# Prompt attention: TensorE multiplies the values of the item two back before it turns the weights of the last item

## Chip, core and metric

The kernel runs on one core of one Trainium2 chip. The metric is the device time of one execution in microseconds (us), as the median of several executions. One execution was also recorded by the hardware profiler, and every row below comes from that one.

## What is computed

The program is one layer of a decoder: a projection, two attention branches, their merge, and a mixture of experts, for a prompt of 512 tokens and a sample group of 32 tokens. The change touches only the attention of the prompt. Cut to that:

```python
# branch a: 8 query heads, 2 key/value heads, the top keys of an index score are kept
logits = einsum('bqgrd,bqkgd->bqgrk', qg, k_sel) * HEAD_DIM ** -0.5
p = softmax(where(valid, logits, -inf));  o_a = einsum('bqgrk,bqkgd->bqgrd', p, v_sel)
# branch b: 8 query heads, 8 key/value heads, blocks of 256 keys, causal inside the own block
p = softmax(concatenate([s_sel, s_own]));  o_b = p_own @ v_own + p_sel @ v_sel
```

With 512 keys the kernel treats both as dense attention with an additive mask: the index scores (with the dropped keys lowered) for branch a, a causal triangle for branch b. HEAD_DIM is 64, and a tile of queries has 128 rows.

## The kernel before

The program is a sequence of stages, each a block of instruction streams for the five engines, and a stage starts when all engines have ended the one before. `prompt` is the attention of the prompt; `project` is ahead of it, and `sample`, `merge`, `project_out` and `experts` are behind it. No instruction of another stage runs on an engine while `prompt` runs.

`prompt` works through 32 items. An item is one pair of heads (j = 0 to 3) of one branch ("b" or "a") for one tile of 128 queries (t). Four items make a group, which shares one output bank and one normalisation. The groups are, in order, b3, a3, b2, a2, b1, a1, b0, a0: the tile t = 3 sees 512 keys, t = 2 sees 384, t = 1 sees 256 and t = 0 sees 128, so items get shorter. Group g holds the items 4g to 4g+3.

The steps of an item m, by short names that the rest of the document uses:

- S(m), TensorE, line 1042: the scores of both heads (`scores`), into one of two pairs of banks.
- D(m), VectorE, lines 1145 and 1148: adds the mask and takes the row maximum.
- E(m), ScalarE, line 1104: the exponentials of both heads, with their sums. D(m) releases it.
- T(m), TensorE, line 1055: turns the weights (`turn`), 2(t+1) transposes of 128x128 into banks 4 and 5. It needs E(m), and the banks empty again, that is K(m-1).
- K(m), ScalarE (line 1114 for a b item, 1116 for an a item) and for b items VectorE too (line 1167): copies the turned weights out of the banks to `probT`. It needs T(m).
- W(m), TensorE, line 1069: multiplies the values with the turned weights (`weigh`), 2(t+1) products into bank 6. It needs K(m); the first item of a group also needs N of the group before, which empties bank 6.

Per group g there are four more:

- I(g), VectorE, line 1152: the reciprocals of the sums.
- P(g), TensorE, line 1081: spreads the reciprocals over the rows of bank 7 by 8 products (`spread`).
- X(g), ScalarE, line 1122: copies them out.
- N(g), VectorE, line 1158: multiplies bank 6 by them and writes the output; it needs X(g) and the group's last W.

Each engine runs its stream in the order in which it is written, and semaphores order the engines among each other. ScalarE's order in turn m of the loop is E(m), K(m-1), and X(g) behind K(m-1) where m = 4g+5. VectorE's is D(m), the copy of K(m-1) for a b item, I(g) where m = 4g+4, N(g) where m = 4g+5. GpSimd issues loads for the next stage when certain exponentials have been made. TensorE's order is what the diff changes.

Of the kernel before, what the change touches and what calls it, by code (L numbers as in the profile page):

```python
# [176 lines left out]
def const(s, name, rows=P):  # L177
    a, n = AT[name]
    return s.consts[0:rows, a:a + n]


def build(nc, a, o):

    with ExitStack() as ctx:
# [18 lines left out]
        with ExitStack() as attn:  # L203
# [7 lines left out]
            with ExitStack() as samp:  # L211
# [10 lines left out]
                with ExitStack() as qkv:  # L222
                    def sq(name, shape, dt=F32):
                        return qkv.enter_context(nc.sbuf_tensor(name, shape, dt, side="right"))
                    s.qaT = sq("qaT", [P, PAIRS, SEQ])
                    s.qbT = sq("qbT", [P, PAIRS, SEQ])
                    s.kbT = sq("kbT", [P, PAIRS, SEQ])
                    s.vbP = sq("vbP", [P, TP, H, HD])
                    s.vaP = sq("vaP", [P, TP, 2, HD])
                    s.score = sq("score", [P, TP, SEQ])  # L230
                    with nc.cleanup_on_exit():
                        project(nc, s, a, o)

                    s.oaT = sa("oaT", [P, PAIRS, NTOK])
                    s.obT = sa("obT", [P, PAIRS, NTOK])
                    s.bw = sa("branch_w", [P, 2, 2, PAIRS, P])
                    s.ring = samp.enter_context(nc.sbuf_tensor("ring", [P, NR, SLOT_B * QW], F32))
                    with nc.cleanup_on_exit():  # L238
                        prompt(nc, s, a)
# [726 lines left out]
def prompt(nc, s, a):  # L966
# [4 lines left out]
    with ExitStack() as ctx:  # L971
# [19 lines left out]
        n = len(ITEMS)  # L991

        def width(t):
            return (t + 1) * P


        def by_scalar(m):
            return sum(1 if item[1] == "b" else 2 for item in ITEMS[:m])

        def by_vector(m):  # L1000
            return sum(item[1] == "b" for item in ITEMS[:m])

        @block.gpsimd
        def _(pool):
            link = Chain(pool, queries_laid)
            keys = a["cache_k_idx"][0].rearrange("g (p e) d -> (g p) (e d)", e=SLOT)
            for half in range(2):
                r = slice(half * HD, half * HD + HD)
                link(nc.gpsimd.tensor_copy(s.q_a[r, :, half * 16:half * 16 + 16].rearrange("p b (j q) -> p b j q", q=NQ),
                                           s.qaS[r, :, :].rearrange("p j (b q) -> p b j q", q=NQ)))  # L1010
                for j in range(PAIRS):
                    c = (2 * j + half) * NQ
                    link(nc.gpsimd.tensor_copy(s.q_b[r, :, j, c:c + NQ], s.qbS[r, j, :].rearrange("p (b q) -> p b q", q=NQ)))
                for odd in range(2):
                    dst = s.q_i[r, :, :].rearrange("p b (j a q) -> p a b j q", a=2, q=NQ)
                    src = s.qiS[odd * HD:(odd + 1) * HD, :, :].rearrange("p j (b q) -> p b j q", q=NQ)
                    link(nc.gpsimd.tensor_copy(dst[:, odd, :, :, :], src))

            for k in range(NIDX):
                for u in range(4):  # L1020
                    b, f = 4 * (k // 2) + u, k % 2
                    pool.wait_ge(exp_done, 2 * (4 * k + u + 1))
                    pool.indirect_dma_start(s.ring[:, k, u * SLOT * HD:(u + 1) * SLOT * HD], None, keys,
                                            bass.IndirectOffsetOnAxis(s.rows[:, 2 * b + f:2 * b + f + 1], 0))\
                        .then_inc(s.arrived[k], 16)
            for n in range(NR - NIDX):
                pool.wait_ge(exp_done, 2 * (4 * NIDX + 3 * n + 2))
                gather_unit(pool, s, a, n)

        @block.tensor  # L1030
        def _(pe):
            ident = const(s, "ident")

            def scores(m):
                _, kind, t, j = ITEMS[m]
                if m >= 2:
                    pe.wait_ge(exp_done, 2 * (m - 1))
                for half in range(2):
                    r = slice(half * HD, half * HD + HD)
                    qT = s.qaT if kind == "a" else s.qbT  # L1040
                    kT = s.kaT[r, 0:width(t)] if kind == "a" else s.kbT[r, j, 0:width(t)]
                    last = nc.tensor.matmul(bank[:, 2 * (m % 2) + half, 0:width(t)], qT[r, j, t * P:(t + 1) * P], kT,
                                            start=True, stop=True)
                last.then_inc(qk_done, 1)

            def turn(m):
                t = ITEMS[m][2]
                pe.wait_ge(exp_done, 2 * (m + 1))
                for half in range(2):
                    if m >= 1:  # L1050
                        pe.wait_ge(tr_kept, by_scalar(m))
                    if by_vector(m):
                        pe.wait_ge(tr_kept_v, by_vector(m))
                    for c in range(t + 1):
                        last = nc.tensor.transpose(bank[:, 4 + half, c * P:(c + 1) * P],  # L1055
                                                   prob[:, m % 3, half, c * P:(c + 1) * P], ident)
                last.then_inc(tr_done, 1)

            def weigh(m):
                g, kind, t, j = ITEMS[m]  # L1060
                pe.wait_ge(tr_kept, by_scalar(m + 1))
                if by_vector(m + 1):
                    pe.wait_ge(tr_kept_v, by_vector(m + 1))
                if j == 0 and g >= 1:
                    pe.wait_ge(out_kept, g)
                for c in range(t + 1):
                    for half in range(2):
                        v = s.vaP[:, c, half, :] if kind == "a" else s.vbP[:, c, 2 * j + half, :]
                        last = nc.tensor.matmul(bank[half * HD:half * HD + HD, 6, j * P:(j + 1) * P], v,
                                                probT[:, m % 2, half, c * P:(c + 1) * P],  # L1070
                                                start=(c == 0), stop=(c == t))
                last.then_inc(weighed, 1)

            def spread(g):

                pe.wait_ge(inv_ready, g + 1)
                if g >= 1:
                    pe.wait_ge(wide_kept, g)
                for j in range(PAIRS):
                    for half in range(2):  # L1080
                        last = nc.tensor.matmul(bank[half * HD:half * HD + HD, 7, j * P:(j + 1) * P],
                                                inv[:, g % 2, j, half:half + 1].to_broadcast([P, HD]), ident,
                                                start=True, stop=True)
                last.then_inc(wide_done, 1)

            for m in range(n + 2):
                if m < n:
                    scores(m)
                if 1 <= m < n + 1:
                    turn(m - 1)  # L1090
                if m >= 2:
                    if (m - 1) % PAIRS == 0:
                        spread((m - 1) // PAIRS - 1)
                    weigh(m - 2)

        @block.scalar
        def _(act):
            def exps(m):
                g, _, t, j = ITEMS[m]
                for half in range(2):  # L1100
                    act.wait_ge(top_done, m + 1)
                    if m >= 3:
                        act.wait_ge(tr_done, m - 2)
                    nc.scalar.activation(prob[:, m % 3, half, 0:width(t)], bank[:, 2 * (m % 2) + half, 0:width(t)],  # L1104
                                         ACT.Exp, bias=ntop[:, m % 4, half:half + 1],
                                         accum_out=sums[:, g % 2, j, half:half + 1]).then_inc(exp_done, 1)

            def keep_turned(m):
                _, kind, t, _ = ITEMS[m]
                act.wait_ge(tr_done, m + 1)  # L1110
                if m >= 2:
                    act.wait_ge(weighed, m - 1)
                if kind == "b":
                    nc.scalar.copy(probT[:, m % 2, 0, 0:width(t)], bank[:, 4, 0:width(t)]).then_inc(tr_kept, 1)
                else:
                    nc.scalar.copy(probT[:, m % 2, :, 0:width(t)], bank[:, 4:6, 0:width(t)]).then_inc(tr_kept, 2)
# [1536 lines left out]
```

## Time and profile before

| | |
|---|---|
| median of 3 executions | 1060.63 us (1059.89 to 1061.24) |
| the profiled execution: its time | 1053.66 us |
| the profiled execution: first to last instruction | 1051.9 us |
| `prompt`, first score product to last normalisation | 183.62 to 286.90 us |
| TensorE busy over the span | 907.5 us, 86% |

The profiled execution was 7 us shorter than the median of the others, so durations are taken from the profile and differences are applied to the median. The profile shows an engine's instructions in order of time with their durations, and, in brackets, how long the engine had been idle and which engine's instruction released it. A TensorE row that stands for several matmuls gives the time from the start of the first to the end of the last; the next burst can start some 0.1 us before that end, as they are pipelined. (TensorE makes an fp32 product in passes, so the trace has twice as many matmuls as the program in S, W and P.)

### The profile page before, as it was taken

How to read it: one execution, taken by the hardware profiler on the slowest of the kernel's cores; microseconds unless marked ns; L12 is line 12 of the kernel's file. 1: busy time of each engine (PE TensorE's matmuls, PEld its weight loads, DVE VectorE, ACT ScalarE, POOL GpSimd, SP SyncE). 2: the span in 40 equal slices, each digit the busy share in tenths (PEclk: the TensorE clock that was granted, in tenths of full speed). 3: DMA queues.
4: the chain of work that ended last, by engine and by line, in shares of the span. 5: the costliest groups of instructions: out<-in, count | busy, mean ns of one | idle time of the engine just before them, and what ended most of it. 6: DMA issues, size and time to landing. Idle time of an engine off the chain costs nothing. (4 is left out here: it accounts for less than half of the span.)

```text
span 1051.9 us, 14867 instructions
## 1 busy us (share of the span) xinstructions
PE 907.5 (86%) x5957; PEld 581.6 (55%) x5957; DVE 429.8 (41%) x906; ACT 303.1 (29%) x542; POOL 198.6 (19%) x214
## 2 busy tenths in 40 slices
PE   6999998878699999989979999999659999777750
PEld 4775886555566666534669999744533444322220
DVE  4728996656428595312035422111341111111106
ACT  5435332455536776621300000011201111100002
POOL 0333330321012334423510000000111111011010
PEclk9999999899989999999989999999759999999995
DMA  9220221223267997999956550195359999999946
GB/s 327 94 92 1 94 71 43 61 61 117 85 221 261 341 372 306 356 411 354 395 185 177 184 185 21 26 341 205 109 206 395 414 413 413 414 413 414 404 167 238
DMA packets 87844, 246.87 MB, mean 235 GB/s; under 512 B 13088, under 2 KB 40928, under 8 KB 75360
## 3 DMA queue, kind: packets, MB, share of 16 engines
q1 hardware_dynamic: 66448, 144.45, 37.0%
q0 software_dynamic: 20560, 99.24, 25.0%
q10 hardware_dynamic: 768, 2.23, 0.6%
q8 instruction: 48, 0.79, 0.3%
q14 instruction: 20, 0.16, 0.0%
HBM read 238.50 MB, written 15.77 MB: 242 GB/s over the span
## 5 line engine op out<-in xcount | busy, mean ns | idle before, releaser
L1337 PEld LDWEIGHTS bank<-consts,ring 128*128 128x128 f32 x704 | 78.1, 143 | 38.6 <-ACT kT_s L1580 36.3
L1580 ACT COPY kT_s<-bank 128x1024 f32<-128x1024 f32 (+1 forms) x90 | 85.5, 996 | 45.7 <-PE bank L1337 45.7
L2357 PE MATMUL bank<-early,obT 128*64 128x512 f32 x352 | 82.0, 614 | 14.6 <-DMA early<-in_w_e_up 13.3
L1337 PE MATMUL bank<-consts,ring 128*128 128x128 f32 x704 | 89.5, 281 | 2.4 <-PEq L238 1.9
L2565 DVE TENSOR_TENSOR uT<-uT,bank 128x256 f32<-128x256 f32 x16 | 6.7, 421 | 182.2 <-ACT uT L2414 182.2
L491 POOL TENSOR_TENSOR w_lo<-w_raw,w_hi 128x512 fp32r<-128x512 f32 x37 | 49.1, 1329 | 105.0 <-ACT w_hi L534 105.0
L878 PE MATMUL bank<-w_hi,hT_hi_p 128*128 128x512 f32 x160 | 65.4, 408 | 0.0
L2357 PEld LDWEIGHTS bank<-early,obT 128*64 128x64 f32 x352 | 27.7, 141 | 66.8 <-issue 53.3
L878 PE MATMUL bank<-w_lo,hT_hi_p 128*128 128x512 f32 x160 | 62.5, 391 | 0.0
L878 PE MATMUL bank<-w_hi,hT_lo_p 128*128 128x512 f32 x160 | 62.4, 390 | 0.0
L2010 PE MATMUL bank<-w_o,uT 128*128 128x512 f32 x128 | 55.6, 593 | 2.6 <-PEq L251 2.6
L1831 PE MATMUL bank<-hT_hi,gate_w_hi 128*128 128x272 f32 x192 | 56.5, 294 | 0.0
L1831 PE MATMUL bank<-hT_hi,gate_w_lo 128*128 128x272 f32 x192 | 55.4, 288 | 0.0
L1831 PE MATMUL bank<-hT_lo,gate_w_hi 128*128 128x272 f32 x192 | 55.3, 288 | 0.0
L294 POOL DMA_INDIRECT ring<-in_cache_k_b,rows_b x32 | 30.0, 937 | 113.2 <-PE bank L1337 88.0
L2287 POOL DMA_INDIRECT expert_rows<-branch_w,ids x15 | 15.2, 1016 | 191.0 <-ACT branch_w L2418 191.0
L1860 ACT ACTIVATE sig<-bank 128x544 f32<-128x544 f32 x12 | 7.5, 625 | 138.5 <-PE bank L1831 138.5
L2414 ACT ACTIVATE uT<-bank 128x256 f32<-128x256 f32 x16 | 6.1, 383 | 139.2 <-PE bank L2357 139.2
L1104 ACT ACTIVATE prob<-bank,ntop 128x512 f32<-128x512 f32 (+3 forms) x64 | 33.1, 522 | 42.5 <-DVE ntop L1148 42.2
L1458 PE MATMUL bank<-ring,kT_s 128*32 128x512 f32 (+1 forms) x512 | 39.6, 461 | 6.2 <-DMA ring<-in_cache_v_a,rows 3.0
L2418 ACT COPY branch_w<-bank 128x1024 f32<-128x1024 f32 x16 | 16.2, 1012 | 95.7 <-PE bank L2379 95.7
L1055 PE MATMUL bank<-consts,prob 128*128 128x128 f32 x160 | 25.7, 295 | 19.2 <-ACT prob L1104 11.5
(384 smaller groups left out, 1693.8 us busy)
## 6 DMA issues: line engine op xcount, KB each, us to landing
early<-in_w_e_gate SPq DMA_DIRECT2D x44, 512.0 KB, 13.8
early<-in_w_e_up SPq DMA_DIRECT2D x44, 512.0 KB, 16.5
early<-in_w_e_down SPq DMA_DIRECT2D x12, 1024.0 KB, 13.7
w_raw<-in_w_in SPq DMA_DIRECT2D x10, 1024.0 KB, 7.4
early_gates<-in_w_e_down SPq DMA_DIRECT2D x10, 1024.0 KB, 19.0
w_o<-in_w_e_gate SPq DMA_DIRECT2D x20, 512.0 KB, 13.5
w_o<-in_w_e_up SPq DMA_DIRECT2D x20, 512.0 KB, 15.8
uT<-in_w_e_down SPq DMA_DIRECT2D x10, 1024.0 KB, 14.5
```

Of the source, the lines that this page charges most:

```text
L294: pool.indirect_dma_start(s.ring[:, r, at:at + wide], None, cache.rearrange("g (p e) h d -> (g p) (e h d)", e=e), bass.IndirectOffsetOnAxi ...
L491: nc.gpsimd.tensor_tensor(w_lo[:, k, :].bitcast(F32R), raw_w(gi, k), w_hi[:, k, :], ALU.subtract)\
L878: last = nc.tensor.matmul(bank[:, n % 4, :], l, m, start=(k == 0 and c == 0), stop=(k == KD - 1 and c == 2))
L1055: last = nc.tensor.transpose(bank[:, 4 + half, c * P:(c + 1) * P], prob[:, m % 3, half, c * P:(c + 1) * P], ident)
L1104: nc.scalar.activation(prob[:, m % 3, half, 0:width(t)], bank[:, 2 * (m % 2) + half, 0:width(t)], ACT.Exp, bias=ntop[:, m % 4, half:half + 1],
L1337: last = nc.tensor.transpose(bank[:, u, e * P:(e + 1) * P], ring[:, slot, at:at + P], ident)
L1458: last = nc.tensor.matmul(out[rows_at(u), :], probT[m][:, c * nslot + e, rows_at(u)], ring[:, slot, base + e * w:base + (e + 1) * w], star ...
L1580: nc.scalar.copy(kT[:, n % 2, u, :], bank[:, u, :]).then_inc(kT_kept, 1)
L1831: last = nc.tensor.matmul(out, l, m, start=(k == 0 and c == 0), stop=(k == KD - 1 and c == 2))
L2010: last = nc.tensor.matmul(bank[:, n % 4, :], uT[:, k, t * P:(t + 1) * P], wo[:, k, half * 512:half * 512 + 512], start=(k == 0), stop=(k = ...
L2357: last = nc.tensor.matmul(bank[half(u), 2, :].rearrange("r (c n) -> r c n", c=2), xT[:, slot % 2, k, half(u)], gate_up_at(s, slot)[:, u, : ...
L2418: nc.scalar.copy(y[:, slot % 2, :].rearrange("p (b n) -> p b n", b=2), bank[:, 4 + 2 * (slot % 2):6 + 2 * (slot % 2), :]).then_inc(y_ready, 1)
```

## The change

In the loop over turns, T(m-1) moves from ahead of P and W(m-2) to behind them. Nothing is added or taken away, and no wait of any step changes.

```diff
             for m in range(n + 2):
                 if m < n:
                     scores(m)
-                if 1 <= m < n + 1:
-                    turn(m - 1)
                 if m >= 2:
                     if (m - 1) % PAIRS == 0:
                         spread((m - 1) // PAIRS - 1)
                     weigh(m - 2)
+                if 1 <= m < n + 1:
+                    turn(m - 1)
```

The streams of the other four engines stay as they are. On TensorE the first place is the end of the first group: T(4), P(0), W(3), S(6), T(5), W(4), S(7) before.

```order
L1055 MATMUL bank<-consts,prob 128x128 x8
L1081 MATMUL bank<-consts,inv 64x128 x8
L1069 MATMUL bank<-probT,vbP 64x128 x8
L1042 MATMUL bank<-early_gates,qaT 128x512 x2
L1055 MATMUL bank<-consts,prob 128x128 x8
L1069 MATMUL bank<-probT,vaP 64x128 x8
L1042 MATMUL bank<-early_gates,qaT 128x512 x2
```

The same place on TensorE now: P(0), W(3), T(4), S(6), W(4), T(5), S(7).

```order
L1081 MATMUL bank<-consts,inv 64x128 x8
L1069 MATMUL bank<-probT,vbP 64x128 x8
L1055 MATMUL bank<-consts,prob 128x128 x8
L1042 MATMUL bank<-early_gates,qaT 128x512 x2
L1069 MATMUL bank<-probT,vaP 64x128 x8
L1055 MATMUL bank<-consts,prob 128x128 x8
L1042 MATMUL bank<-early_gates,qaT 128x512 x2
```

T(4) has moved behind both P(0) and W(3), and T(5) behind W(4), the product that needs N(0); the scores keep their distance.

The second place on TensorE is the end of group 5 (a1): T(23), W(22), S(25), T(24), P(5), W(23), S(26), T(25), W(24) before.

```order
L1055 MATMUL bank<-consts,prob 128x128 x4
L1069 MATMUL bank<-probT,vaP 64x128 x4
L1042 MATMUL bank<-kbT,qbT 128x128 x2
L1055 MATMUL bank<-consts,prob 128x128 x2
L1081 MATMUL bank<-consts,inv 64x128 x8
L1069 MATMUL bank<-probT,vaP 64x128 x4
L1042 MATMUL bank<-kbT,qbT 128x128 x2
L1055 MATMUL bank<-consts,prob 128x128 x2
L1069 MATMUL bank<-probT,vbP 64x128 x2
```

The same place on TensorE now: W(22), T(23), S(25), P(5), W(23), T(24), S(26), W(24), T(25).

```order
L1069 MATMUL bank<-probT,vaP 64x128 x4
L1055 MATMUL bank<-consts,prob 128x128 x4
L1042 MATMUL bank<-kbT,qbT 128x128 x2
L1081 MATMUL bank<-consts,inv 64x128 x8
L1069 MATMUL bank<-probT,vaP 64x128 x4
L1055 MATMUL bank<-consts,prob 128x128 x2
L1042 MATMUL bank<-kbT,qbT 128x128 x2
L1069 MATMUL bank<-probT,vbP 64x128 x2
L1055 MATMUL bank<-consts,prob 128x128 x2
```

T(24), which stood directly behind S(25), now stands behind P(5) and W(23).

## Rows read from the trace of the kernel before

**Rows 1.** Windows: stage, us, busy per engine (instructions), TensorE clock, DMA share, GB/s.

```profile
183.60:287.70 104.10, 82.04 (x736) 54.87 (x736) 59.30 (x96) 56.15 (x169) 22.46 (x34) 0.94 0.25 82
287.70:754.00 466.30, 446.75 (x3144) 308.52 (x3144) 170.65 (x315) 139.22 (x174) 91.56 (x100) 0.97 0.68 246
754.00:1051.90 297.90, 210.15 (x1000) 89.41 (x1000) 73.68 (x153) 32.71 (x52) 33.98 (x36) 0.90 0.89 351
```

**Rows 2.** Waits in 183 to 288 us: us in total, times, longest.

```profile
PE bank L1055 <- ACT prob L1104: 11.5, 9, 2.6
...
PE bank L1055 <- ACT probT L1114: 6.6, 7, 1.3
```

**Rows 3.** Timeline at the first group's end: start us, duration us, instruction, idle before.

```profile
204.62 1.09 PE L1081 MATMUL bank<-consts,inv 128*64 128x128 f32 x16
...
206.51 1.13 PE L1042 MATMUL bank<-early_gates,qaT 64*128 64x512 f32 x4
207.77 1.06 PE L1055 MATMUL bank<-consts,prob 128*128 128x128 f32 x8
209.03 1.09 PE L1069 MATMUL bank<-probT,vaP 128*64 128x128 f32 x16 [0.20 <-DVE obT L1158]
210.06 1.13 PE L1042 MATMUL bank<-early_gates,qaT 64*128 64x512 f32 x4
213.77 1.91 PE L1055 MATMUL bank<-consts,prob 128*128 128x128 f32 x8 [2.58 <-ACT prob L1104]
...
206.66 1.01 ACT L1116 COPY probT<-bank 128x1024 f32<-128x1024 f32 x1
207.56 0.60 ACT L1122 COPY inv_wide<-bank 128x512 f32<-128x512 f32 x1
...
208.19 0.69 DVE L1158 TENSOR_TENSOR obT<-bank,inv_wide 128x512 f32<-128x512 f32 x1 [2.90 <-ACT inv_wide L1122]
208.80 1.22 DVE L1145 TENSOR_TENSOR bank<-bank,score 128x1024 f32<-128x1024 f32 x1
```

**Rows 4.** Timeline from N(4) to N(5), group a1.

```profile
261.01 0.69 DVE L1158 TENSOR_TENSOR obT<-bank,inv_wide 128x512 f32<-128x512 f32 x1 [2.05 <-ACT inv_wide L1122]
261.22 0.66 PE L1055 MATMUL bank<-consts,prob 128*128 128x128 f32 x4
...
261.85 0.66 PE L1069 MATMUL bank<-probT,vaP 128*64 128x128 f32 x8
...
262.44 0.70 PE L1042 MATMUL bank<-early_gates,qaT 64*128 64x256 f32 x4
...
263.19 0.70 DVE L1145 TENSOR_TENSOR bank<-bank,score 128x512 f32<-128x512 f32 x1 [0.15 <-PE bank L1042]
...
264.65 0.47 ACT L1104 ACTIVATE prob<-bank,ntop 128x256 f32<-128x256 f32 x1
...
265.56 0.58 ACT L1116 COPY probT<-bank 128x512 f32<-128x512 f32 x1
...
267.40 0.49 PE L1042 MATMUL bank<-kbT,qbT 64*128 64x128 f32 x4
...
269.01 1.09 PE L1081 MATMUL bank<-consts,inv 128*64 128x128 f32 x16
...
269.57 0.26 ACT L1114 COPY probT<-bank 128x128 f32<-128x128 f32 x1
...
269.93 0.61 PE L1069 MATMUL bank<-probT,vaP 128*64 128x128 f32 x8
270.15 0.58 ACT L1122 COPY inv_wide<-bank 128x512 f32<-128x512 f32 x1 [0.32 <-PE bank L1081]
270.77 0.69 DVE L1158 TENSOR_TENSOR oaT<-bank,inv_wide 128x512 f32<-128x512 f32 x1 [1.36 <-ACT inv_wide L1122]
```

**Rows 5.** Timeline: the stage's last instruction, N(7).

```profile
286.21 0.69 DVE L1158 TENSOR_TENSOR oaT<-bank,inv_wide 128x512 f32<-128x512 f32 x1 [3.78 <-ACT inv_wide L1122]
```

**Rows 6.** Window behind TensorE's longest idle time; columns as in rows 1.

```profile
214.00:216.00 2.00, 2.00 (x12) 1.67 (x12) 0.00 (x0) 1.45 (x5) 0.53 (x1) 0.50 0.50 131
```

## Prediction

> **What bounds the kernel now.** I read the windows by stage first. `prompt` fills 104 of the 1051.9 us, and TensorE, its busiest engine, works in 82 of them; the stage behind is TensorE's (446.75 busy of 466.30), and the last works at 0.89 of its DMA engines [rows 1]. A stage starts when all engines have left the one before, so what `prompt` gains or loses moves all that follows: I carry it one to one. The first place where it could be swallowed is a stage in which TensorE already has 96% of the time, which leaves little room.
>
> Next the waits inside `prompt`. TensorE's idle time sits almost all ahead of T: 11.5 us put down to the exponentials and 6.6 us to the copy of the turned weights [rows 2]. That is the 18 us a change of order could fill, if the step now put first could start earlier than T can. So the question is what releases W(m-2). It needs K(m-2), and T(m-1) needs E(m-1) and the same K(m-2). On ScalarE K(m-2) stands behind E(m-1). So by the time W(m-2) may start, T(m-1) may start too: T(m-1) has no condition that W(m-2) lacks in effect. T(6) waited 2.58 us [rows 3]; the row names the exponentials, but K(5) stands behind E(6), so that W(5) in its place would wait exactly as long. No W fills a wait. The one step that does come free is P(g): it needs only I(g), and now runs inside the wait.
>
> **The change part by part.** Nothing is added or removed; bursts trade places. In a turn of the loop TensorE did T, (P), W, S; now it does (P), W, T, S. Three things follow.
>
> 1. *S keeps its place in ordinary turns*: ahead of it stand the same bursts. Price nothing, gain nothing. What hides this is that both orders wait for the same copy.
>
> 2. *T comes later by one W.* That is 1.03 us in a t = 3 item (209.03 to 210.06 [rows 3]) and 0.59 us in a t = 1 item (261.85 to 262.44 [rows 4]). K(m) starts at the later of T(m)'s end and E(m+1)'s end, so most of it is covered: T(5) ended at 208.83, while ScalarE released T(6) only at 213.77 [rows 3], behind E(6) and K(5). T(5) could have come 1 us later and nobody would have waited. If all 32 delays were exposed, the sum over tiles would be about 22 us (8 x (1.0 + 0.8 + 0.6 + 0.4), of which the ends are the two measured here); the waits named above say that E and K, not T, come last, so I don't take this end.
>
> 3. *At a group's end two waits move.* W(4g+4) needs N(g). Before, T(4g+5) ran while N(g) was made: T(5) 207.77, then N(0) 208.19 to 208.88, then W(4) 209.03, S(7) 210.06 [rows 3]. Now W(4) stands ahead: it still starts at 209.03 at best, then T(5) at 210.06, then S(7) at 211.1, one T later. And T(4g+4), next group's first item, stands behind P(g) and W(4g+3). K(4g+4) waits for it, and X(g) stands behind K(4g+4) on ScalarE, N(g) behind X(g).
>
> I work one group's end out in full, N(4) to N(5), 9.76 us before (261.01 to 270.77 [rows 4]). A burst shown as 0.66 us was followed by the next after 0.59 (261.85, 262.44), the 0.49 us score burst I follow after 0.42 on the same grounds, and P(5) by W(23) after 0.92. Release costs 0.03 us. New order: N(4) ends 261.70; W(20) 261.73; T(21) 262.32; S(23) 262.91; D(23) 0.75 later, as before (262.44 to 263.19), at 263.66; E(23) 1.46 later, 265.12; K(22) 0.91 later, 266.03, done 266.61; W(22) 266.64; T(23) 267.23; S(25) 267.82; P(5) 268.24; W(23) 269.16; T(24) 269.75, done about 0.42 later, 270.17; K(24) 270.20; X(5) behind it by its 0.26 less the 0.1 overlap of ScalarE (206.66 + 1.01 to 207.56 [rows 3]), 270.36; N(5) 0.62 later (270.15 to 270.77), 270.98. That is 0.2 us more than before. Before, K(24) at 269.57 was early and P(5), at 269.01, came last; now P(5) is early and K(24) comes last. The stall did not go; it changed its name.
>
> The same walk with each tile's own durations through all 32 items gives, for the old order, the last normalisation ending at 286.98 us against 286.90 in the trace [rows 5], starts of E within 0.3 us of the trace all the way, and for the new order 288.6. By group, the end N(g) comes later by 0, 0.3, -0.1, 0.5, 0.2, 0.4, 0 and 0.4 us: 1.6 us in sum. The losses fall on the ends of a groups; at the ends of b groups P inside the wait gives back what T loses. As the walk makes the interval of N(4) to N(5) 0.36 longer and the rows 0.2, I put the sum between 1.1 and 2.0.
>
> Against the profiled execution this is 1053.66 + 1.6 = 1055.3. That execution was 7 us below the median of the runs, for which this trace has no reason, so I put the difference on the median: 1060.63 + 1.6 = 1062.2.
>
> **The rivals.**
>
> *Nothing measurable, because the clock gives it back* (2 in 10). Behind the 2.58 us wait, T(6) ran at half the clock: 1.91 us against 1.06 for T(5), granted clock 0.50 [rows 3, 6], that is 1.2 of 2.4 GHz. W(5) behind it lay in the same window; at 0.85 us each they cost 1.7 us. In the new order S(7) ends 1 us later and the idle time ahead of that burst shrinks to about 1.6 us. If the clock then doesn't fall, 1.6 - 1.7 leaves nothing, 1060.5. The page "TensorE: Matmul & The Clock Gate" of the Trainium skill (part 1) says the activity check runs freely, not tied to the program, so that the same kernel meets it at different places. By that a shift of one microsecond may as well switch a half-speed stretch on as off.
>
> *More than forecast, because it falls once more* (2 in 10). The mean clock of the stage is 0.94 [rows 1], so few bursts are slow now. If a burst of two steps at t = 2 meets half clock behind one of the later waits, by the ratio 1.91 to 1.06 it costs 0.8 x (0.8 + 0.8) = 1.3 us and 2.9 in all: 1063.5. That is slower by 0.27%. The idle time grows nowhere in the walk by over 1 us, which speaks against more than one.
>
> *Faster: P(g) out of the way* (1 in 12). P(g) and W(4g+3) now run up to 0.9 us earlier, and S(4g+6) with them: by the walk at 205.6 where it was at 206.51 [rows 3]. Were D(4g+6) waiting for these scores, each of 7 group ends would give 0.8 us: -5.6, 1055.0. The point that decides is what VectorE does just ahead of D(6). In the rows D(6) at 208.80 follows N(0) without idle time, and N(0) had waited 2.90 us for X(0) [rows 3]. X(0) at 207.56 follows K(4) at 206.66, though P(0) had ended at 205.71. So the early scores lie unused. The Trainium skill, "PSUM — Partial Sum Buffer", section "Engine vs sequencer instructions", calls ScalarE's queue strictly first in, first out, and matmuls too start in program order. By this rule X can't pass K, nor T(5) pass a waiting W(4); the trace agrees, with X(0) 1.85 us behind P(0)'s end. If instead X(5) could pass K(24), it would start at P(5)'s end, 268.24 + 1.09, and N(5) at 269.98, 0.8 us earlier than before rather than 0.2 later.
>
> *The forecast itself* has the rest, a little over half, with 1.1 to 2.0 us more. A part lost or added behind `prompt`, where the last stage waits for DMA, belongs to its spread; I allow 0.8 us either way.
>
> **How the numbers follow.** A measurement of this kernel can tell about 0.2%, 2.1 us, from no change. Forecast (0.52): three quarters under 2.1 us, a quarter over, as its two uncertainties add. Clock gives back (0.20): same. Clock falls again (0.20): four fifths slower. Faster (0.08): faster. Together: slower 0.13 + 0.16 = 0.29, same 0.39 + 0.20 + 0.04 = 0.63, faster 0.08. The range leaves out the faster case and the far tail of the third: from 1059.7, the first rival with 0.8 us of spread, to 1064.3, the third case with as much.
>
> **What would show it.** In the new profile T should start about one W after the W that now stands ahead, and that W should carry the waits that T carried, 18 us, put down to E or K. P(0) should start near 202.7 and S(6) near 205.6, and D(6) should not move. At the end of an a group X should start directly behind K(4g+4), not behind P. S(7) should come 1 us later. `prompt` should end 1.6 us later than before, and the stages behind should keep their lengths. Clock rows around 213 us tell the first two rivals apart. I am wrong if some W runs before T could have, that is if a W starts while ScalarE is still in E(m-1); if the end of `prompt` moves by over 3 us; or if it moves as forecast and the total does not.

## The result, and the profile after

| | before | after |
|---|---|---|
| median of 6 executions each, run together | 1060.26 us (1055.2 to 1063.59) | 1068.61 us (1064.87 to 1073.18) |
| the profiled execution: its time | 1053.66 us | 1067.51 us |
| its span, mean granted clock | 1051.9 us, 0.952 | 1065.7 us, 0.946 |

The changed kernel is slower: the ratio is 1.0095, with a 95% interval of 1.0066 to 1.0123. That is 8.4 us by the medians and 10 by the ratio, where I had forecast 1.6, and outside my range. All ratios leave out executions that took over 1.5% more than the fastest of their kernel, while the medians count them.

The windows of the new profile by stage: `prompt`, the first and the second half of `sample` (up to the first scores of line 1432, and from there). Columns as in rows 1.

```profile
183.60:288.70 105.10, 81.83 (x736) 53.18 (x736) 60.24 (x96) 56.51 (x169) 22.45 (x34) 0.94 0.26 81
288.70:438.20 149.50, 145.08 (x1212) 92.26 (x1212) 88.44 (x193) 96.12 (x109) 48.72 (x51) 0.98 0.81 294
438.20:553.20 115.00, 103.16 (x796) 57.10 (x792) 18.17 (x28) 24.23 (x28) 39.05 (x42) 0.92 0.87 336
```

`prompt` took 105.1 us against 104.1 [rows 1], so in this pair of executions only 1.0 of 13.8 us lies in the stage that was changed. The same two halves of `sample` took 146.7 and 108.7 us before: 9.1 us lie there, in a stage whose code is the same, and most of the rest in the last one (295.3 us for 292.1). Two single executions can't tell whether that is the change or chance; the experiments and their profiles are there for it.

Inside `prompt` the new timeline can be held against the forecast step by step. At the first group's end (compare rows 3):

```profile
202.76 1.09 PE L1081 MATMUL bank<-consts,inv 128*64 128x128 f32 x16
...
205.68 1.13 PE L1042 MATMUL bank<-early_gates,qaT 64*128 64x512 f32 x4
...
208.88 1.22 DVE L1145 TENSOR_TENSOR bank<-bank,score 128x1024 f32<-128x1024 f32 x1
209.11 1.09 PE L1069 MATMUL bank<-probT,vaP 128*64 128x128 f32 x16 [2.30 <-DVE obT L1158]
210.13 1.09 PE L1055 MATMUL bank<-consts,prob 128*128 128x128 f32 x8
211.15 1.13 PE L1042 MATMUL bank<-early_gates,qaT 64*128 64x512 f32 x4
...
213.79 1.10 PE L1069 MATMUL bank<-probT,vaP 128*64 128x128 f32 x16 [1.51 <-ACT probT L1116]
214.82 1.09 PE L1055 MATMUL bank<-consts,prob 128*128 128x128 f32 x8
```

P(0) starts at 202.76 and S(6) at 205.68, D(6) behind it does not gain (208.88 against 208.80). W(4) waits for N(0) until 209.11. T(5) stands behind it now and comes at 210.13, 2.4 us later than before, and S(7) at 211.15, 1.1 us later. W(5) now stands first behind the idle time, which is down to 1.51 us, and it and T(6) take 1.10 and 1.09 us: full clock, 2.4 GHz. The half-speed stretch of rows 6 is gone, as in my first rival.

At the end of group a1 (compare rows 4):

```profile
261.08 0.69 DVE L1158 TENSOR_TENSOR obT<-bank,inv_wide 128x512 f32<-128x512 f32 x1 [2.05 <-ACT inv_wide L1122]
...
268.45 1.09 PE L1081 MATMUL bank<-consts,inv 128*64 128x128 f32 x16
...
269.91 0.44 PE L1055 MATMUL bank<-consts,prob 128*128 128x128 f32 x2
...
270.38 0.27 ACT L1114 COPY probT<-bank 128x128 f32<-128x128 f32 x1
...
270.55 0.59 ACT L1122 COPY inv_wide<-bank 128x512 f32<-128x512 f32 x1
271.17 0.69 DVE L1158 TENSOR_TENSOR oaT<-bank,inv_wide 128x512 f32<-128x512 f32 x1 [0.49 <-ACT inv_wide L1122]
```

N(4) to N(5) is 10.09 us against 9.76. P(5) ends at 269.54, but X(5) starts only at 270.55, directly behind K(24): the stall changed its name, as forecast. TensorE's waits in 183 to 288 us (us in total, times, longest) now stand almost all at W, line 1069; the largest other one inside the stage is the last line (compare rows 2):

```profile
PE bank L1069 <- DVE obT L1158: 7.2, 4, 2.3
PE bank L1069 <- ACT probT L1116: 5.7, 7, 1.5
...
PE bank L1069 <- DVE oaT L1158: 3.4, 3, 1.2
PE bank L1069 <- ACT probT L1114: 2.7, 7, 0.6
PE bank L1055 <- ACT prob L1104: 1.8, 1, 1.8
```

These are 19.0 us at W where T had 18.1. But 10.6 of them are waits for N, seven in number, one per group end, where I had expected E or K. In sum no idle time was filled; it was cut into other pieces.

### The profile page after: what moved, and what is told of

Read it like the earlier page. It is cut to its first block and busy times, and to the rows that moved or that the text cites. A ratio compares the mean times of both kernels' runs of the same rounds, so it can differ in the third digit from the quotient of the medians.

```text
span 1065.7 us, 14867 instructions
## 1 busy us (share of the span) xinstructions
PE 916.2 (86%) x5957; PEld 582.8 (55%) x5957; DVE 430.7 (40%) x906; ACT 303.7 (28%) x542; POOL 199.0 (19%) x214
## 5 line engine op out<-in xcount | busy, mean ns | idle before, releaser
L491 POOL TENSOR_TENSOR w_lo<-w_raw,w_hi 128x512 fp32r<-128x512 f32 x37 | 49.1, 1329 | 105.1 <-ACT w_hi L534 105.1
L1458 PE MATMUL bank<-ring,kT_s 128*32 128x512 f32 (+1 forms) x512 | 42.8, 470 | 5.4 <-issue 3.8
L294 POOL DMA_INDIRECT ring<-in_cache_v_b,rows_b x32 | 30.6, 955 | 63.2 <-PE bank L1458 40.6
```

The lines of the kernel that those rows point to most:

```text
L294: pool.indirect_dma_start(s.ring[:, r, at:at + wide], None, cache.rearrange("g (p e) h d -> (g p) (e h d)", e=e), bass.IndirectOffsetOnAxi ...
L491: nc.gpsimd.tensor_tensor(w_lo[:, k, :].bitcast(F32R), raw_w(gi, k), w_hi[:, k, :], ALU.subtract)\
L1458: last = nc.tensor.matmul(out[rows_at(u), :], probT[m][:, c * nslot + e, rows_at(u)], ring[:, slot, base + e * w:base + (e + 1) * w], star ...
```

## The experiments

Each kernel was timed in five rounds, in turn with the kernel before on the same chip, and each ratio is to that kernel. Chips differ: the kernel before had medians of 1053.26, 1058.15, 1059.25, 1059.54 and 1059.62 us in the five series. Within a series its executions spread widely (1045.25 to 1060.82 us in the first), so one execution says little. "Cut" kernels end early and leave out every stage behind the cut, outputs included; for them the differences in us count. Where such kernels ran on different chips, I compare their ratios, and turn a difference of ratios into us by the kernel before (0.001 is 1.06 us).

In the traces I read one measure: N(0) to N(7), from the start of the first row of line 1158 to that of the last. It is 78.02 us before (208.19 to 286.21 [rows 3, 5]) and 78.96 after (208.27 to 287.23).

### Series 1: is it the change, and is it the later end?

`c1_same_order` is the kernel before, built again; `c2_new_order` is the changed one. Two more keep the old order and end `prompt` later by work that TensorE does ahead of the last spread; the work only fills a bank that is free.

```diff
+                if m == n + 1:
+                    for extra in range(8):      # e2: range(24)
+                        nc.tensor.transpose(bank[:, 0, extra % 4 * P:(extra % 4 + 1) * P], ident, ident)
```

> The kernel before, unchanged, as a control and for a second profile of it. Theory A (the 8 us lie in stages behind the attention and belong to how a single execution falls) expects a spread of some 8 us that reaches the times of the changed kernel, and a profile that may lose time where the changed one did. Theories B and C expect 1055 to 1064 us and a ratio of 1.000 within 0.003.

> The changed kernel, unchanged, for a second profile. Theory A expects a mean that comes closer to the old order's. Theories B and C expect 1065 to 1073 us again, with the loss again behind the attention: about 1 us at its end, 9 to 10 us at the end of the sample stage.

> Old order; 8 transposes into a free bank, written ahead of the last spread, so that the prompt attention ends 1 to 2 us later and is otherwise as before. Theory B (a later start of the sample stage is amplified by what follows) expects 1066 to 1070 us. Theory C (the new order itself does it, not the lateness of the end) and theory A expect 1 to 2 us more than before, 1061 to 1063.

> As the one before with 24 transposes: the prompt attention ends 3 to 5 us later. Theory B expects at least 8 us more in all, 1068 us or over. Theories A and C expect the delay itself, 1063 to 1066 us.

| run | median | ratio, interval |
|---|---|---|
| c1_same_order | 1053.88 us | 1.0011 [0.9978, 1.0045] |
| c2_new_order | 1059.77 us | 1.0058 [1.0028, 1.0087] |
| e1_end_1us_later | 1059.09 us | 1.0039 [1.0009, 1.0069] |
| e2_end_3us_later | 1056.75 us | 1.0026 [0.9998, 1.0053] |

The control is equal, the new order slower again: it is the change, not scatter. That a later end is amplified behind `prompt` fell: in the profiles `prompt` takes 108.8 us in e2 against 102.4 in c1, and e2's total is only 2.9 us longer by the medians, 1.6 by the ratios. e1 is no clean test of a later end. Its `prompt` takes 107.1 us, but 4.4 of the 4.7 us over c1 were lost by N(6) (N(0) to N(6) is 73.33 us for 68.91), ahead of the work that was added. That is a finding of its own, because up to there e1 is the old order. Its TensorE was at half clock too, from 275.16 us until shortly before 282, at bursts that take 0.44 and 1.09 us at full clock:

```profile
275.16 0.70 PE L1069 MATMUL bank<-probT,vbP 128*64 128x128 f32 x4
...
279.21 1.98 PE L1081 MATMUL bank<-consts,inv 128*64 128x128 f32 x16
```

The profile of `c2_new_order` shows what that of the changed kernel had shown only at its very end. Its windows over the last items, those with 128 keys:

```profile
276.00:283.00 7.00, 5.92 (x40) 4.11 (x40) 2.40 (x6) 2.75 (x11) 0.00 (x0) 0.50 0.20 84
283.00:290.00 7.00, 4.76 (x32) 2.96 (x30) 1.67 (x4) 2.03 (x7) 0.00 (x0) 0.50 0.00 0
```

And the same two windows of `c1_same_order`, in the old order:

```profile
276.00:283.00 7.00, 5.15 (x50) 3.87 (x48) 2.52 (x6) 3.09 (x12) 0.00 (x0) 0.87 0.05 21
283.00:290.00 7.00, 5.25 (x52) 4.52 (x56) 1.29 (x5) 3.42 (x5) 0.94 (x1) 0.89 0.33 88
```

The first column behind the window's length is TensorE's busy time with its instructions, the third from the right the granted clock. (From 285.56 us on `c1_same_order` is already in `sample`.) In the new order it stands at 0.50, 1.2 GHz, for 14 us on end; TensorE looks busier (5.92 against 5.15 us) and does less (40 matmuls against 50). The timeline of `c2_new_order` at that place:

```profile
270.80 0.44 PE L1069 MATMUL bank<-probT,vbP 128*64 128x128 f32 x4 [1.24 <-DVE oaT L1158]
...
272.50 0.44 PE L1069 MATMUL bank<-probT,vbP 128*64 128x128 f32 x4 [0.47 <-ACT probT L1114]
272.87 0.44 PE L1055 MATMUL bank<-consts,prob 128*128 128x128 f32 x2
273.24 0.80 PE L1042 MATMUL bank<-early_gates,qaT 64*128 64x128 f32 x4
274.02 0.70 PE L1069 MATMUL bank<-probT,vbP 128*64 128x128 f32 x4
...
276.00 1.97 PE L1081 MATMUL bank<-consts,inv 128*64 128x128 f32 x16
...
280.83 0.70 PE L1069 MATMUL bank<-probT,vaP 128*64 128x128 f32 x4 [1.08 <-DVE obT L1158]
...
286.21 1.98 PE L1081 MATMUL bank<-consts,inv 128*64 128x128 f32 x16
```

At 273.24 a score burst that took 0.49 us takes 0.80. From there W takes 0.70 instead of 0.44 and P 1.97 instead of 1.09. From 262 us to the end of `prompt` no idle time of TensorE is longer than 1.24 us; at the border to `sample`, still at half clock, one of 1.76 us follows. Nor does the longest idle time decide: the changed kernel's profile has one of 1.39 us ahead of 280.02 and its clock held until about 282.

### Series 2: how much is already there when `prompt` ends?

The two orders, cut behind `prompt` and behind `sample`:

```diff
+                if True:
+                    return
                 with nc.cleanup_on_exit():
                     sample(nc, s, a)
```

> Old order, and the program ends behind the prompt attention: the sample attention, the merge, the output projection and the experts are left out. The reference for the next run; some 290 us.

> New order, cut at the same place. The prediction's walk expects 1.1 to 2.0 us more than the cut old order. The two pairs of profiles so far (104.1 and 102.4 us old, 105.1 and 106.1 us new for the stage) expect 2.4 us. Theory C (the whole 6 to 8 us come from the order inside this stage) expects 6 us or more. A difference under 1 us would mean that the stage's own loss is noise of its half-speed stretches.

> Old order, and the program ends behind the sample attention: the merge, the output projection and the experts are left out. The reference for the next run; some 540 us.

> New order, cut at the same place. Theory B (the sample stage, which loads from the cache at the rate that DMA gives, makes more of a late start) expects 5 to 8 us more than the cut old order. If what was lost at the prompt attention is only carried on, 1 to 3 us.

| run | median | ratio, interval | N(0) to N(7) |
|---|---|---|---|
| t1_old_to_prompt | 290.33 us | 0.2735 [0.272, 0.275] | 76.40 us |
| t2_new_to_prompt | 294.9 us | 0.2786 [0.2775, 0.2797] | 81.77 us |
| t3_old_to_sample | 550.35 us | 0.5202 [0.5186, 0.5218] | 78.03 us |
| t4_new_to_sample | 556.89 us | 0.5251 [0.523, 0.5273] | 81.80 us |

By the medians, 4.6 us of the loss are there when `prompt` ends and 6.5 when `sample` ends; by the ratios it is 5.4 (0.0051) and 5.2 (0.0049), and the two profiles differ by 5.37 us from N(0) to N(7). With 0.0015 to either side of one ratio being 1.6 us, the loss at the end of `prompt` is about 5 us, three times my 1.6, and nothing shows that `sample` adds to it. The granted clock of 274 to 294 us tells the orders apart. The old order cut behind `prompt`:

```profile
274.00:294.00 20.00, 8.50 (x78) 6.12 (x77) 5.14 (x13) 5.72 (x23) 0.00 (x0) 0.91 0.15 54
```

The new order cut at the same place:

```profile
274.00:294.00 20.00, 14.22 (x90) 9.01 (x88) 6.47 (x16) 7.21 (x32) 0.94 (x1) 0.54 0.14 53
```

Over all profiles of the two orders the clock of this window is 0.79, 0.91, 0.91 and 0.91 in the old one (before, c1, t1, t3) and 0.74, 0.51, 0.54, 0.56 and 0.50 in the new one (after, c2, t2, t4, f1). The changed kernel's own profile was the mildest of five. The two kernels of series 1 with added work, which are in the old order as well, read 0.83 (e1) and 0.79 (e2) there, and e1 was at half clock in the midst of it.

### Series 3: which items, and is it the clock?

`p1_new_long_items` has the new order only in turns below 25 (items with 256 keys and more), `p2_new_short_items` only from there on. `p3_new_filled` has it everywhere, and in the turns of the short items multiplies a constant into a free bank while TensorE would wait (where that bank is the turned weights' own, it first waits for their copy, as T itself does). `p4_spread_first` moves only P ahead of T and leaves W behind it. All are cut behind `prompt`. In the edits, `fill(b, k)` makes k transposes of the identity into bank b.

```diff
+                if m >= 25 and m <= n:
+                    if m % PAIRS in (3, 0):
+                        fill(7, 3)
+                    elif m % PAIRS == 2:
+                        pe.wait_ge(tr_kept, by_scalar(m - 1))
+                        pe.wait_ge(tr_kept_v, by_vector(m - 1))
+                        fill(4, 6)
```

> The program ends behind the prompt attention (all later stages left out). New order in the first 25 turns of the loop, which hold the items with 512, 384 and 256 keys; old order from there on. The cut old and new orders took 290.3 and 294.9 us. Theory D (the order costs what the walk says, and the rest is half speed that the new order brings in the groups with 128 keys, as three of its four profiles show from 273 to 294 us) expects the walk's 1.2 us and no long stretch at half speed: 291.5. Theory E (each swapped turn costs the same) expects 24 of 32 parts of 4.6: 293.8.

> Cut at the same place. Old order in the first 25 turns, new order from turn 25 on, which are the items with 128 keys. Theory D expects 0.3 us from the walk and about 3 from a half-speed stretch that begins between 273 and 276 us: 293.5. Theory E expects 8 of 32 parts of 4.6: 291.5.

> Cut at the same place. New order in all turns; in the turns of the items with 128 keys TensorE makes 3 or 6 transposes of the identity into a bank that is free just then, ahead of the waits, so that it idles less. Theory D expects the clock to stay up until 282 us or so and 292 to 293 us, though work was added. If the clock is not the cause, the fillers cost or leave the time: 295 us or more.

> Cut at the same place. Only the spread of the reciprocals goes ahead of the turn; turn and values keep the old order. The walk expects 1.1 us less than the old order, 289.2, as the spread lies inside a wait. If early spreads lie unused, as the prediction said of the faster rival, 290.3.

| run | median | ratio, interval |
|---|---|---|
| p1_new_long_items | 292.63 us | 0.2763 [0.275, 0.2775] |
| p2_new_short_items | 291.94 us | 0.2757 [0.2744, 0.277] |
| p3_new_filled | 292.16 us | 0.2752 [0.274, 0.2765] |
| p4_spread_first | 289.59 us | 0.2722 [0.2707, 0.2738] |

By the ratios the two parts lose 3.0 and 2.3 us against t1, together 5.3 of the 5.4; each of these differences is uncertain by some 2 us, so neither part can be shown to carry the loss alone. The profile of p1 is worth a look: its items with 128 keys are in the old order, and still TensorE ran from 276 to 283 us at a clock of 0.51. The fillers bring the new order from 294.9 to 292.16 us, by the ratios 3.6 us less, though they add work to TensorE. The windows of p3 show why:

```profile
276.00:283.00 7.00, 6.84 (x65) 4.57 (x63) 3.92 (x12) 4.56 (x21) 0.94 (x1) 1.00 0.41 150
283.00:290.00 7.00, 5.29 (x52) 3.39 (x50) 2.85 (x7) 3.10 (x12) 0.00 (x0) 1.00 0.00 1
```

The clock stays at 1.00 where it was 0.50. (Its profile has two other slow stretches, near 211 and near 221 us, ahead of the fillers, which take part of the gain back: N(0) to N(1) takes 18.84 us there and 15.70 in t2.) P alone moved ahead (p4) ends 0.7 us earlier than the old order by the medians and 1.4 by the ratios, which the intervals don't tell from nothing.

The fillers could have helped in another way than by the clock, for example by moving the waits. N(5) to N(6), a group with 128 keys, speaks against it: it takes 8.01 us in the changed kernel's profile, where that group ran at full clock without fillers, 8.13 in p3 and f2 with them, and 10.02 or 10.03 in c2, t2, t4 and f1, where the clock fell inside it.

### Series 4: the same in the whole program

> The changed kernel whole, as the reference on this chip for the three beside it: 6 to 8 us over the kernel before.

> The new order with transposes of the identity as fillers in the turns of the items with 128 keys, now in the whole program. Cut behind the prompt attention it took 2.7 us less than the new order without them. If the half-speed stretch there is also what the sample stage inherits, at least 3 us less than the changed kernel beside it, and up to 5. If what the sample stage loses has another cause, 2.7 us less at most.

> Only the spread ahead of the turn, whole program. The walk expects 1.1 us less than before, the cut run showed 0.7 less. Within 2 us of the kernel before either way.

> Spread ahead of the turn, and in the turns that wait longest (the third behind each group's end) 6 or 12 transposes of the identity into the free bank 7, ahead of the wait. If half speed behind long waits is a cost of its own, this saves the 1.7 us of the stretch at 214 us and some of the one at the end: 2 to 4 us less than before. If TensorE's fillers only get in the way, no gain over the run without them.

The last kernel's loop, in which the fillers stand behind the scores of every fourth turn:

```diff
                 if m < n:
                     scores(m)
+                if m < n and m >= 7 and m % PAIRS == 3:
+                    fill(7, 12 if m == 7 else 6)
+                if m >= 2 and (m - 1) % PAIRS == 0:
+                    spread((m - 1) // PAIRS - 1)
                 if 1 <= m < n + 1:
                     turn(m - 1)
                 if m >= 2:
-                    if (m - 1) % PAIRS == 0:
-                        spread((m - 1) // PAIRS - 1)
                     weigh(m - 2)
```

| run | median | ratio, interval | N(0) to N(7) |
|---|---|---|---|
| f1_new_order_full | 1066.56 us | 1.0073 [1.0045, 1.01] | 81.79 us |
| f2_new_filled_full | 1062.38 us | 1.0035 [1.0012, 1.0058] | 77.71 us |
| f3_spread_first_full | 1057.5 us | 0.9996 [0.9973, 1.002] | 76.27 us |
| f4_spread_first_filled_full | 1055.54 us | 0.996 [0.9941, 0.9979] | 73.82 us |

The new order is slower a third time. Fillers give back 4.2 us of 1066.56, and N(0) to N(7) falls by 4.08 us: the gain in the whole program is of the size of that in `prompt`. P ahead of T alone can't be told from no change. With fillers it is faster than both kernels.

### Series 5: the same fillers in all three orders

> The whole program in the old order (T, P, W), with transposes of a constant behind the scores of every fourth turn (12 in turn 7, 6 in turns 11 to 31), all in waits of TensorE; they change no output. It asks whether what the best version won belongs to the fillers or to the place of the spread. If the half-speed stretches cost the old order too (its profiles show 7 to 10 us of them in the attention), filling removes some and the ratio is 0.996 to 0.998. If the gain needs the early spread, the ratio is 0.999 to 1.002.

> The whole program in the new order (P, W, T) with the same transposes. If the fillers are worth the same whatever the order, it stands above the filled old order by what the new order costs at full clock, some 2.6 us, so the ratio is 0.999 to 1.001. If the half-speed stretch of the last items, which the new order has at nearly every execution, isn't met by these places, it stays at 1.003 or more.

| order | without fillers | with the fillers of f4 | N(0) to N(7) with them |
|---|---|---|---|
| T, P, W (before) | 1.0011 [0.9978, 1.0045] | 0.9974 [0.9953, 0.9996] | 75.41 us |
| P, W, T (the change) | 1.0073 [1.0045, 1.01] | 1.0001 [0.9979, 1.0022] | 79.88 us |
| P, T, W | 0.9996 [0.9973, 1.002] | 0.996 [0.9941, 0.9979] | 73.82 us |

In the old order the fillers are worth 0.26%, the distance of 0.9974 from the kernel before itself. In the third order they are worth 0.36%, on one chip. In the new order f2's are worth 0.38% on one chip, and those of f4 some 0.7%, where the two kernels ran on different chips. So most of what f4 won belongs to the fillers, not to the place of P. On one chip the new order with fillers stands 2.5 us above the old one with them (1060.2 against 1057.72 us), 2.9 by the ratios. They didn't free it of half clock: in the profile of `g2_new_order_same_fill_full` the last spread still runs slow.

```profile
281.32 1.26 PE L1088 MATMUL bank<-consts 128*128 128x128 f32 x6
282.51 0.70 PE L1069 MATMUL bank<-probT,vaP 128*64 128x128 f32 x4
...
285.58 1.98 PE L1081 MATMUL bank<-consts,inv 128*64 128x128 f32 x16
```

In `f2_new_filled_full`, with the fillers made for the short items, the same spread runs at full clock:

```profile
284.21 1.09 PE L1081 MATMUL bank<-consts,inv 128*64 128x128 f32 x16
```

And so it does in the filled old order, `g1_old_order_filled_full`:

```profile
282.85 1.04 PE L1081 MATMUL bank<-consts,inv 128*64 128x128 f32 x16
```

The granted clock of both profiles is 1.00 all the way from 208 us to N(7), so they give each order at full clock: 75.41 and 77.71 us from N(0) to N(7). The difference of 2.30 us is what the order costs by itself (to some 0.1 us, since the fillers cost a little: N(4) to N(5) is 9.89 us in g1 and 9.76 in rows 4).

## Why the prediction was wrong

**What was right.** The reason why no W could fill a wait held: no W ran before T could have. So did the places of P(0), S(6), W(4), T(5) and S(7), within 0.1 us; that D(6) gains nothing; that ahead of X(5) K(24) takes the place of P(5); and the direction, slower. The sentence that the Trainium skill gave ("PSUM — Partial Sum Buffer", section "Engine vs sequencer instructions") on strict order held as well: X(5) waited for K(24) 1.01 us behind the end of P(5).

**The term "1.6 us" was too small.** At full clock it is 2.30 us from N(0) to N(7). By group the filled kernels give (g1 against f2, N to N):

| N(0)–N(1) | –N(2) | –N(3) | –N(4) | –N(5) | –N(6) | –N(7) |
|---|---|---|---|---|---|---|
| 15.11 / 15.70 | 13.38 / 13.54 | 12.37 / 12.88 | 10.39 / 10.70 | 9.89 / 10.09 | 7.95 / 8.13 | 6.32 / 6.67 |
| +0.59 | +0.16 | +0.51 | +0.31 | +0.20 | +0.18 | +0.35 |
| forecast 0.3 | -0.1 | 0.5 | 0.2 | 0.4 | 0 | 0.4 |

The ends of the a groups (first, third, fifth and seventh interval) lose 1.65 us in sum where I had 1.6, though a3 loses twice what I gave it. The ends of the b groups lose 0.65 us where I had 0.1: P inside the wait gives back less than T loses. (My eight numbers add up to 1.7, from which I wrote 1.6; that is rounding.) With 2.3 in place of 1.6 the forecast would have been 1062.9 us: still inside the range.

**The step that failed is the clock.** My sum put it at nothing. My two rivals on it were one stretch given back (-1.7 us) and one burst of two steps slowed (+1.3 us), and I argued against more by "the idle time grows nowhere in the walk by over 1 us". Both happened, but the second at another size and place. The stretch at 214 us is absent in every profile of the new order (f1, c2, t2, t4, after); but it is absent in two of six of the old one as well (c1, t1), and p3, which is in the new order without fillers there, was at half clock near 211 and near 221 us. In its place TensorE runs at half clock over the items with 128 keys, from 273 to 276 us to the end of `prompt` in four of five profiles, some 16 us. The old order's N(0) to N(7) averages 77.14 us over four profiles (78.02, 76.10, 76.40, 78.03), which is 1.7 over its full-clock 75.41; the new order's averages 81.22 over five (78.96, 81.80, 81.77, 81.80, 81.79), 3.5 over its 77.71. So half clock costs the new order 1.8 us more than the old, net of what was given back. With e1 and e2 counted as old order up to N(6), that stretch averages 70.47 us in the old order and 72.52 in the new, 1.4 and 1.5 over full clock (69.09 and 71.04), and only the last group differs, by 1.0 us; so the net is 1.0 to 1.8 us. With the 2.3 that makes 3.3 to 4.1, a forecast of 1063.9 to 1064.7 us at the upper end of my range, against about 5 measured with the cut kernels. Shown by intervention is that half clock costs the new order time, since work added in the waits took 2.7 us (p3) and 4.2 us (f2) away. The exact share isn't, and part of the whole loss stays without an account.

Why the clock falls so much earlier in the new order stays open, and so does whether the order decides it: e1 fell at 275 us in the old order, and p1 at 276 us in items in the old order. It is not plain chance where: in c2, f1, t2 and t4 the fall came in the same burst, S(28), 3.3 us behind the start of N(5) each time (273.24, 274.05, 275.31 and 276.24 us), and in e1 and p1 one burst before and one behind S(28). The sum of TensorE's idle time doesn't tell it (18.1 us at T before, 19.0 at W after), nor how busy it is just ahead of the short items: in 262 to 276 us it worked 10.29 and 10.43 us in the old order (before, c1) and 10.61 in the changed kernel's profile, where the clock didn't fall until 282. That little idle time is added, my argument against more, decided nothing.

**"I carry it one to one" is neither shown nor refuted.** My sign of being wrong, that the end of `prompt` moves by over 3 us, came true. In the whole program the new order lost 0.58, 0.73 and 0.95%, that is 6 to 10 us with about 3 to either side of each, and the cut kernels show 5.4 us at the end of `prompt` and 5.2 at the end of `sample`. The 6 and 8 us fit that within their error; the 10 of the first comparison don't need to, and I have no account for what they hold beyond. "The stages behind should keep their lengths" failed in the changed kernel's profile, where `sample` took 9.1 us more. But in twelve whole-program profiles whose code is the same there, `sample` took 254.3 to 265.2 us: 264.5 in the changed kernel's, 257.7 in c2's, and 263.4 in g1's, which has the old order. The five profiles of the old order average 257.4 us and the five of the new one 261.7. Such a spread can't tell whether the order has a part in it. Nor does N(0) to N(7) tell the total: against 77.14 us, f2 is 0.6 us longer there and loses 3.7 us by its ratio, g2 is 2.7 longer and loses 0.1.

**The chances.** Slower by over 0.2% had 0.29. The part of it that held the answer, "falls once more", had 2 in 10 with a price from one burst. The profile of before had more to say than I took from it: besides the stretch of rows 6, the clock is 0.74 in 283 to 290 us and 0.59 in 290 to 297, across the end of `prompt` and into `sample`. The price belonged to the whole last groups, not to one burst.

## What to carry to other kernels

Swapping two steps that are released by the same event fills no wait; follow what stands behind each on the other engines, and charge every group end its own loss. Before calling a small reorder harmless, price TensorE at half clock over the whole stretch in which short bursts alternate with waits, even if the sum of its idle time stays. If such a stretch exists, cheap work put into the waits can be worth more than the order: here it gave 0.3 to 0.4% against kernels of the same series. And take several profiles of either order: one profile of each would have shown the stretch or missed it by chance.

## What the hardware showed beyond expectation

- TensorE stayed at 1.2 GHz for 14 us and more while it was busy 5.92 of 7 and 4.76 of 7 us. By the bursts (0.70 us for 0.44, 1.97 for 1.09) the same work at full clock would keep it less busy, so the busy share hides the state; the matmul counts (40 against 50 in 276 to 283 us) show it. The page "TensorE: Matmul & The Clock Gate" of the Trainium skill, in its section "A second HAM failure mode: psum-queue depth-cycling", says that frequent short idle times between groups of products can make the clock swing between its levels. The trace agrees so far as the clock fell with no idle time over 1.24 us from 262 us on, and work put into the waits kept it up in p3. But in c2 it did not swing, it stayed low to the end of `prompt`.
- 6 transposes of a constant in every fourth turn (12 in the first), 48 in all, made the unchanged order faster: 0.9974 [0.9953, 0.9996], though the interval ends close to 1.
- The fall goes with the order but isn't tied to it: with the same instructions and nearly the same idle time, 274 to 294 us ran at 0.79 to 0.91 in four profiles of one order and at 0.50 to 0.56 in four of five profiles of the other. Yet e1, in the old order, was at half clock for over 6 us of it.
